# Boundaries between sub-layers by halves of the tokens in a two-layer diffusion trunk: down projection in two passes, first six gate/up blocks per half

## What is computed

```python
def swiglu(h, wg, wu, wd):
    return (jax.nn.silu(h @ wg) * (h @ wu)) @ wd

def modulate(x, g_pre, shift, scale):
    return (rmsnorm(x, g_pre) * (1 + scale[:, None]) + shift[:, None])

def add_residual(x, y, g_post, gate, weight):
    return (x + weight * gate[:, None] * rmsnorm(y, g_post))

# one sub-layer, for context and latent tokens with their own shift, scale, gate
xc = add_residual(xc, swiglu(modulate(xc, g[0], mc[:, 0], mc[:, 1]), wg, wu, wd), g[1], mc[:, 2], 0.5)
```

## Time and profile before

| | us |
|---|---|
| median of 3 runs | 2836.14 |
| lowest and highest | 2830.37, 2842.32 |
| the profiled execution's own time | 2835.41 |
| its span, first to last instruction | 2833.6 |
| mean granted TensorE clock | 0.968 |

### The profile page before, as it was taken

One profiled execution on the slowest core, in us unless ns is written; L12 is line 12 of the kernel. 1 busy time (PEld: TensorE's weight loads), 2 busy tenths in 40 slices (PEclk: granted clock), 3 DMA queues, 4 the chain that ended last, 5 costly groups with the idle time before them and its releaser, 6 DMA issues.

```text
span 2833.6 us, 41253 instructions
## 1 busy us (share of the span) xinstructions
PE 2661.6 (94%) x17263; PEld 2552.0 (90%) x17263; DVE 1301.7 (46%) x2002; ACT 905.4 (32%) x1294; POOL 3.7 (0%) x5
## 2 busy tenths in 40 slices
PE   6999999898887889999998999999889999999997
PEld 6999999785676889999988999998878888999997
DVE  6888321533436377752136652223665434222222
ACT  4333322444443332222223222222433334333221
POOL 0000000000000000000000000000000000000000
PEclk8999999999987999999999999999989999999999
DMA  6565222120000145532214422222220011222221
GB/s 242 201 208 203 76 78 79 73 74 17 1 5 19 45 174 187 187 113 84 72 45 158 148 104 74 84 72 71 75 64 1 1 53 60 74 74 74 84 77 62
DMA packets 72183, 254.68 MB, mean 90 GB/s; under 512 B 10758, under 2 KB 12822, under 8 KB 71574
## 3 DMA queue, kind: packets, MB, share of 16 engines
q1 hardware_dynamic: 72086, 253.36, 25.7%
HBM read 247.43 MB, written 3.23 MB: 88 GB/s over the span
## 4 chain that ended last, share of the span: by engine, by line
PE 88%; DVE 7%; ACT 3%; issue 1%; DMA 1%; SPq 0%; DVEq 0%; ACTq 0%
PE ps L1940 74%; PE ps L920 2%; PE ps L678 2%; PE ps L538 1%; DVE xT L1911 1%; DVE y L1907 1%; PE ps L1978 1%; PE ps L483 1%; PE ps L906 1%; PE ps L909 1%; PE ps L908 1%; PE ps L1294 0%; ACT w_hi L397 0%; DVE ada_junk L1751 0%; DVE w_lo L403 0%
## 5 line engine op out<-in xcount | busy, mean ns | idle before, releaser
L403 DVE TENSOR_TENSOR w_lo<-w_raw,w_hi 128x1024 fp32r<-128x1024 f32 (+1 forms) x284 | 372.9, 1314 | 1080.3 <-ACT w_hi L397 1080.2
L1940 PE MATMUL ps<-hx_hi,w_hi 128*128 128x320 f32 x3360 | 771.8, 311 | 48.7 <-DVE hx_lo L1808 35.6
L1940 PE MATMUL ps<-hx_lo,w_hi 128*128 128x320 f32 x3360 | 769.0, 310 | 0.0
L1940 PE MATMUL ps<-hx_hi,w_lo 128*128 128x320 f32 x3360 | 768.3, 309 | 0.0
L397 ACT CAST w_hi<-w_raw 128x1024 fp32r<-128x1024 f32 (+1 forms) x284 | 317.9, 1122 | 1328.6 <-PE ps L1940 1273.5
L1940 PEld LDWEIGHTS ps<-hx_hi,w_hi 128*128 128x128 f32 x3360 | 566.6, 189 | 53.5 <-issue 38.8
L1940 PEld LDWEIGHTS ps<-hx_lo,w_hi 128*128 128x128 f32 x3360 | 567.4, 189 | 0.0
L1940 PEld LDWEIGHTS ps<-hx_hi,w_lo 128*128 128x128 f32 x3360 | 566.6, 189 | 0.0
L1940 PE MATMUL ps<-hh_hi,w_lo 128*128 128x320 f32 x1408 | 320.1, 308 | 0.0
L1940 PE MATMUL ps<-hh_hi,w_hi 128*128 128x320 f32 x1408 | 320.1, 308 | 0.0
L1940 PE MATMUL ps<-hh_lo,w_hi 128*128 128x320 f32 x1408 | 320.0, 308 | 0.0
(11 more groups left out here) (280 smaller groups left out, 2246.9 us busy)
## 6 DMA issues: line engine op xcount, KB each, us to landing
w_raw<-in_ffn_gu SPq DMA_DIRECT2D x176, 512.0 KB, 3.2
ring_a<-in_ada_w SPq DMA_DIRECT2D x96, 512.0 KB, 4.4
w_raw<-in_ffn_dn SPq DMA_DIRECT2D x64, 704.0 KB, 4.1
ada_top<-in_ada_w SPq DMA_DIRECT2D x32, 512.0 KB, 5.0
w_raw<-in_even_in SPq DMA_DIRECT2D x16, 512.0 KB, 3.2
w_raw<-in_odd_in SPq DMA_DIRECT2D x12, 512.0 KB, 3.9
first_a<-in_ada_w SPq DMA_DIRECT2D x8, 512.0 KB, 12.2
w_raw<-in_even_out SPq DMA_DIRECT2D x8, 512.0 KB, 3.2
```

Source lines behind the costliest of these rows:

```text
L403: nc.vector.tensor_tensor(w_lo[:, slot, 0:tiles * P], w_raw[:, slot, 0:tiles * P], w_hi[:, slot, 0:tiles * P], ALU.subtract).then_inc(lo_d ...
L1940: last = nc.tensor.matmul(ps[:, out_bank + h, 0:TH], w, a[:, k, h * TH:(h + 1) * TH], start=(start and w is wh and a is hi), stop=(stop an ...
```

## The change

It splits the work around the boundaries by halves of the tokens.

- **Down projection**: two passes over all its weights, first half 0, then half 1 (33 matmuls per chunk, unrolled). Its weights are loaded and split twice. Results rotate through four banks.
- **Boundary chain of half 0** behind a feed-forward: in the second down pass (`chain_tail`): sum of y's squares after its block 0, residual in blocks 1 and 2, squares of x and their sum by block 3, factor and modulation in blocks 4 to 6.
- **Gate/up of the three feed-forwards after the first**: blocks 0 to 5 for half 0 alone, then again for half 1 (12 half-steps, `gu_half`, weights loaded and split twice), then blocks 6 to 21 full. In the first six half-steps the chain of half 1 is spread over ScalarE and VectorE (`chain_first`, `chain_second`, `chain_third`).
- **Into a mixer**, and in the first feed-forward, the first block is done half by half (`in_products`); into a mixer the chain of half 1 runs on TensorE between the two.
- **Behind a mixer** both halves' residual is done, then modulation of half 0; the scale and low operations of half 1 go into half-steps 0 and 1.
- Squares of x go to a buffer of their own with 8 tiles (`xsq`), the scaled x into the same; the output is stored per half; the ada tiles are shared out otherwise (one in each of six half-steps, then three per block), and cond and the first ring of ada tiles are loaded behind half-step 4's weights instead of block 0's; `silu_cond` comes before half-step 6.

```diff
 ADA_RING = 4
-ADA_PLAN = {0: (0, 56, 16), 1: (56, 104, 16), 2: (104, 128, 12)}
+ADA_PLAN = {0: (0, 56), 1: (56, 92), 2: (92, 128)}
+ADA_LAST = 15
+LAG = 6
...
+        def half(h):
+            return slice(h * TH, (h + 1) * TH)
+        def quarter(r):
+            return tmp[:, r // 2, half(r % 2)]
+        def half_groups(h):
+            return ((0, 0, CTX), (1, CTX, TH)) if h == 0 else ((1, TH, T),)
+        def sums_bank(i, h, post):
+            if i and SUBS[i - 1]["kind"] == "ffn":
+                return 1 if h else 4 if post else 5
+            return h
...
+                    for st in range(2 * lag):
+                        for q in range(2):
+                            load(chunk + 2 * st + q, q, ffn_gu[f, st % lag, q], 8)
+                        if st == 4 and f in ADA_PLAN:
+                            sp.wait_ge(x_ready, nth(s["n"] - 1, 1, KT - 1))
+                            load_cond()
+                            ada_begin()
+                        if st >= 2:
+                            ada_loads(st - 2)
...
+                    def chain_first(st, n=n, after=s["after_ffn"]):
+                        if after:
+                            if st == 0:
+                                rms_post(n, 1)
+                            elif st in (1, 2):
+                                squares(n, 1, range(2, 4) if st == 1 else range(6, KT))
+                            elif st == 3:
+                                rms_pre(n, 1)
+                            elif st == 4:
+                                high(n, 1, range(4))
+                        elif st == 1:
+                            high(n, 1, range(4, KT))
+                    def chain_second(st, n=n, after=s["after_ffn"]):
+                        if after:
+                            if st in (0, 1):
+                                squares(n, 1, range(4 * st, 4 * st + 2))
+                            elif st == 4:
+                                high(n, 1, range(4, KT))
+                        elif st == 0:
+                            high(n, 1, range(4))
+                    def gu_half(st, m, h, chunk=chunk, g0=g0):
+                        par = st % 2
+                        split_hi(act, chunk + 2 * st + 2, 0, 8)
+                        chain_first(st)
+                        split_hi(act, chunk + 2 * st + 3, 1, 8)
+                        act.wait_ge(w_used, chunk + 2 * st + 2)
+                        nc.scalar.activation(quarter(2 + par), ps[:, 4 * par + h, 0:TH], ACT.Silu).then_inc(silu_done, 1)
+                        act.wait_ge(mul_done, g0 + st + 1)
+                        nc.scalar.copy(hh_hi[:, m, half(h)], ps[:, 4 * par + 2 + h, 0:TH]).then_inc(hhi_done, 1)
+                        chain_second(st)
...
+                    def chain_tail(b, q, i=n + 1):
+                        if (b, q) == (1, 0):
+                            rms_post(i, 0)
+                        if i == len(SUBS):
+                            return
+                        if (b, q) in ((1, 1), (2, 0), (2, 1), (3, 0)):
+                            r = 2 * (2 * b + q - 3)
+                            squares(i, 0, range(r, r + 2))
+                        elif (b, q) == (4, 0):
+                            rms_pre(i, 0)
+                        elif b == 5:
+                            high(i, 0, range(4 * q, 4 * q + 4))
...
+                    def chain_first(st, n=n, after=s["after_ffn"]):
+                        if after:
+                            if st == 0:
+                                residual(n, 1, range(2))
+                            elif st == 1:
+                                residual(n, 1, range(4, 6))
+                            elif st == 4:
+                                scaled(n, 1, range(4, 6))
+                                low(n, 1, range(2))
+                            elif st == 5:
+                                low(n, 1, range(4, KT))
+                        elif st == 0:
+                            scaled(n, 1, range(4))
+                        elif st == 1:
+                            low(n, 1, range(4))
+                    def chain_second(st, n=n, after=s["after_ffn"]):
+                        if after and st in (0, 1):
+                            scaled_y(n, 1, (4 * st + 2,))
+                    def chain_third(st, n=n, after=s["after_ffn"]):
+                        if after:
+                            if st in (0, 1):
+                                scaled_y(n, 1, (4 * st + 3,))
+                                added(n, 1, (4 * st + 2, 4 * st + 3))
+                            elif st == 3:
+                                scaled(n, 1, range(4))
+                            elif st == 4:
+                                scaled(n, 1, range(6, KT))
+                                low(n, 1, range(2, 4))
+                        elif st == 0:
+                            scaled(n, 1, range(4, KT))
+                        elif st == 1:
+                            low(n, 1, range(4, KT))
+                    def gu_half(st, m, h, chunk=chunk, g0=g0, f=s["f"]):
+                        par = st % 2
+                        up = ps[:, 4 * par + 2 + h, 0:TH]
+                        split_lo(dve, chunk + 2 * st + 2, 0, 8)
+                        chain_first(st)
+                        for j in ada_share(f, st):
+                            ada_step(j)
+                        split_lo(dve, chunk + 2 * st + 3, 1, 8)
+                        dve.wait_ge(silu_done, g0 + st + 1)
+                        nc.vector.tensor_tensor(up, up, quarter(2 + par), ALU.mult).then_inc(mul_done, 1)
+                        chain_second(st)
+                        dve.wait_ge(hhi_done, g0 + st + 1)
+                        nc.vector.tensor_tensor(hh_lo[:, m, half(h)], up, hh_hi[:, m, half(h)].bitcast(F32),
+                                                ALU.subtract).then_inc(block_free, 1)
+                        chain_third(st)
...
+                    def chain_tail(b, q, i=n + 1):
+                        if b in (1, 2):
+                            r = 2 * (2 * b + q - 2)
+                            residual(i, 0, range(r, r + 2))
+                        if i == len(SUBS):
+                            return
+                        if (b, q) in ((4, 1), (5, 0)):
+                            scaled(i, 0, range(4 - 4 * q, 8 - 4 * q))
+                        elif (b, q) in ((5, 1), (6, 0)):
+                            low(i, 0, range(4 - 4 * q, 8 - 4 * q))
                     nc.vector.memset(ssq[:], 0.0).then_inc(ssq_done, 1)
...
+            def half_product(bank, q, hi, lo, k0, tiles, h, first, last_chunk, ready=None, count=True):
+                for t in range(tiles):
+                    if ready is not None:
+                        pe.wait_ge(hx_ready, ready + t)
+                    wh, wl = w_hi[:, q, t * P:(t + 1) * P], w_lo[:, q, t * P:(t + 1) * P]
+                    for w, a in ((wh, hi), (wh, lo), (wl, hi)):
+                        last = nc.tensor.matmul(ps[:, bank, 0:TH], w, a[:, k0 + t, half(h)],
+                                                start=first and t == 0 and w is wh and a is hi,
+                                                stop=last_chunk and t == tiles - 1 and w is wl)
+                if count:
+                    last.then_inc(w_used, 1)
+            def in_products(i, chunk, between=None):
+                for h in range(2):
+                    if h and between:
+                        between()
+                    for q in range(2):
+                        pe.wait_ge(lo_done, chunk + q + 1)
+                        half_product(2 * q + h, q, hx_hi, hx_lo, 0, KT, h, True, True,
+                                     ready=None if q else nth(i, h, 0), count=h == 1)
+            def post_sums(i, h):
+                s = SUBS[i - 1]
+                part = KT * h if s["kind"] == "ffn" else 0
+                sums, newest = (ssq[:], quarter(3)) if s["kind"] == "ffn" else (ssq_m[:, half(h)], sq_m[:, 1, half(h)])
+                out = ps[:, sums_bank(i, h, True), 0:TH]
+                pe.wait_ge(ssq_done, s["ssq0"] + part + KT)
+                pe.wait_ge(sq_ready, s["sq0"] + part + KT)
+                nc.tensor.matmul(out, ones[:], sums, start=True, stop=False)
+                nc.tensor.matmul(out, ones[:], newest, start=False, stop=True).then_inc(msq_ready, 1)
+            def pre_sums(i, h):
+                for k in range(KT):
+                    pe.wait_ge(xsq_ready, nth(i, h, k))
+                    last = nc.tensor.matmul(ps[:, sums_bank(i, h, False), 0:TH], ones[:], xsq[:, k, half(h)],
+                                            start=(k == 0), stop=(k == KT - 1))
+                last.then_inc(xsq_used, 1)
...
+                    def gu_half(st, h, chunk=chunk, g0=g0, n=n, after=after, lag=lag):
+                        par = st % 2
+                        for q in range(2):
+                            pe.wait_ge(lo_done, chunk + 2 * st + q + 1)
```

(24 more changed lines are left out.)

447 lines of the change are left out of this document (247 added, 200 removed).

## The result

| | before | change |
|---|---|---|
| median | 2836.6 us (8 runs) | 2819.2 us (8 runs) |
| lowest and highest | 2830.37, 2855.87 | 2813.09, 2826.96 |
| profiled execution | 2835.4 | 2816.6 |
| its span | 2833.6 | 2814.8 |

The ratio is 0.9933 (95% interval 0.9906 to 0.9959): 0.67% faster, 17.4 us by the medians and 18.8 us by the spans. The forecast was 29.5 us.

A forecast was written before the change was run, and what follows sets the result against it. TensorE, busy 94% of the span, was taken as the bound. Terms: 15.4 + 7.9 + 6.0 + 1.1 + 0.4 + 5.7 - 2.8 - 2.6 - 1.6 = 29.5 us; 2835.4 - 29.5 = 2806 us, range 2791 to 2826.

The forecast's parts named there:

- A: The forecast itself for the whole kernel: 2797 to 2816 us, likeliest 2806; chance 0.58.
- B: Dense half-steps: VectorE and ScalarE don't keep up, 0.5 us in each of 36, 18 us, 2824 us; chance 0.19.
- E: Boundaries into the mixers gain nothing, 0 instead of 7.9 + 6.0, 2820 us; chance 0.05.
- feed-forward to feed-forward: The one boundary between two feed-forwards: 28.0 us instead of 43.35, 15.4 us won.
- end: Behind the last sub-layer only half 1's chain remains: 12.6 us instead of 18.3, 5.7 us won.
- mixer to feed-forward 1, clock included: Boundary behind the even mixer: 0.4 us won after a 2.8 us wait for the burst, less 1.4 us for low clock.
- mixer to feed-forward 3, clock included: Boundary behind the odd mixer: 1.1 us won against 40.83, less 1.4 us for low clock.
- last low part, four times: Down passes: chunk 1 waits 0.65 us for the last low part, four times, 2.6 us lost.
- D: TensorE matmuls: weight loads not hidden when the tile changes, 1984 more changes cost 83 us, 2889 us; chance 0.06.
- C: Half-steps: every stall is covered and the clock comes back at once, 2794 us; chance 0.12.
- the term of 2.8 us for the burst: Feed-forward 1: cond and ada tiles loaded ahead of half-step 5's weights make TensorE wait 2.8 us.
- the clock after a mixer: First half-block after each mixer: second chunk's 24 matmuls at 1.2 GHz cost 2.9 us more; half taken, 1.4 us, twice.

The follow-up runs named there:

- two whole kernels: The change with half-steps undone behind both mixers (2812.9 us, ratio 0.9899), and with half-steps undone in all feed-forwards (2809.2 us, ratio 0.9887).
- spread run: The change with only the first four ada tiles of feed-forwards 1 and 2 moved, one each behind half-steps 5 to 8's weights; 2807.2 us, ratio 0.9898.

## Why the prediction was right or wrong

The direction and the range held: 2819.2 us lies between 2791 and 2826, and faster was right. But the gain was taken 10.6 us too large, and the time lies above the forecast's own likeliest case, A, which ended at 2816. It lies near B (2824) and E (2820), but by the traces B holds only in part and E not at all (below). Term by term, in spans:

| term | forecast | measured |
|---|---|---|
| feed-forward to feed-forward | +15.4 | +14.4 |
| into the even mixer | +7.9 | +7.3 |
| into the odd mixer | +6.0 | +5.5 |
| end | +5.7 | +5.4 |
| mixer to feed-forward 1, clock included | 0.4 - 1.4 = -1.0 | -4.1 |
| mixer to feed-forward 3, clock included | 1.1 - 1.4 = -0.3 | -0.7 |
| last low part, four times | -2.6 | -3.0 |
| start | -1.6 | -2.3 |
| the mixers themselves | 0 | -3.6 |
| sum | 29.5 | 18.9 |

- **Right:** the four large terms, each within 1.0 us, and with them the way of costing them: half-width operations 0.40 to 0.47 us apart, the residual and modulation as one serial chain on VectorE, TensorE free to fill. The end, forecast at 12.6 us with the two sums ahead of T, was 11.8 + 1.1.
- **Right:** the rivals that would have turned the sign. D needed 15 ns more at a change of tile; the narrow down pass runs at 0.1475 us, with 0.1476 already seen outside loops. E is false, both mixer boundaries gained. C is false: the stalls are in the trace. B holds in part: the dense steps stalled by 4.1 us instead of 3.1 between the feed-forwards and did not run away.
- **Wrong, the term of 2.8 us for the burst.** It cost 5.9. The step read from the earlier trace rows that cond, partners, ada tiles and both weight chunks, 4.3 MB, end 12.4 us after the first issue, and put the first chunk's landing 14.9 us after step 3 begins. Measured, it landed after 15.8 us (2.8 to cond's issue, 13.0 from there), and TensorE wanted it at 14.1, the near end of the 14.1 to 14.5 of the forecast: 4.06 us. The step put nothing for the clock behind such a gap, which took 1.8 us more. The spread run gave 5.5 us back.
- **Wrong, the clock after a mixer.** 1.4 us twice were taken for the second chunk of the first half-block at the low clock; those 24 matmuls took 4.0 us behind the even mixer and 4.3 behind the odd one for 3.52, since only the first three to six were 0.27 us apart (1.2 GHz) and the rest 0.147 (2.4 GHz). The case with the low clock through the whole chunk, 2.9 us, did not occur. So the clock was charged where it cost 0.5 to 0.8 us, and not behind the burst, where it cost 1.8.
- **Wrong, the mixers' own time taken as constant.** Nothing in the sum stood for it. It was 3.6 us in the first pair of profiles, and the even one alone took 421 to 443 us over all of them: a scatter that one pair of profiles cannot price.
- **Missed in kind:** the half-steps behind the mixers were costed against the kernel before, not against a first block done half by half, which the two whole kernels show to be 7.0 and 1.1 us shorter. The burst makes 5.5 of the 7.0. In the 1.1 to 1.5 us that are left the wait ahead of half-step 2 has a part, 1.1 us behind the even mixer and 1.4 behind the odd one; the forecast had 1.2 for it. The rest is not told apart.
- **In part luck:** 3.6 us of the 10.6 are the mixers' time in one pair of profiles. In other pairs of the profiles above the even mixer alone differs by -3 to +22 us, so how near the time came to 2806 was not in the forecast's hands to that extent.
